# A mixer's triangular solve with its projections, loads and banks ordered anew, ahead of a mixture of experts

## Time and profile before

| | us |
|---|---|
| median of 3 runs | 1212.01 |
| the profiled execution's own time | 1214.35 |
| its span, first to last instruction | 1212.4 |
| TensorE busy in the span | 1187.4 (98%) |
| VectorE, ScalarE, GpSimd busy | 440.9, 259.5, 44.7 |
| DMA, mean over the span | 360 GB/s |
| TensorE clock granted | 0.998 |

### The profile page before, as it was taken

The page is one execution under the profiler, slowest core; times in us unless marked ns, Lnnn a source line. Parts: engine busy times, 40 slices in busy tenths (PEclk is TensorE's granted clock), DMA queues, the critical chain, the costliest instruction groups (busy, mean ns, idle before and its releaser), DMA issues.

```text
span 1212.4 us, 18239 instructions
## 1 busy us (share of the span) xinstructions
PE 1187.4 (98%) x7814; PEld 572.9 (47%) x7814; DVE 440.9 (36%) x962; ACT 259.5 (21%) x630; POOL 44.7 (4%) x101
## 2 busy tenths in 40 slices
PE   8999999999999999999999999999999999999996
PEld 6777677745344344444443444344444444343332
DVE  3357954753413332332233132313322323232324
ACT  3114435422221111111121212021111111111213
POOL 8000110100000000000000000000000000000000
PEclk9999999999999999999999999999999999999999
DMA  9732302498999999999999999999999999999996
GB/s 285 183 105 71 122 31 72 125 414 334 409 426 429 426 414 428 426 432 431 431 429 431 431 431 432 431 426 431 429 432 432 430 430 431 432 432 428 422 424 231
DMA packets 49387, 436.09 MB, mean 360 GB/s; under 512 B 11525, under 2 KB 26952, under 8 KB 31770
## 3 DMA queue, kind: packets, MB, share of 16 engines
q1 hardware_dynamic: 48180, 431.74, 86.4%
q0 software_dynamic: 960, 3.02, 0.8%
q10 hardware_dynamic: 166, 0.15, 0.0%
HBM read 430.01 MB, written 4.89 MB: 359 GB/s over the span
## 4 chain that ended last, share of the span: by engine, by line
PE 86%; DMA 10%; DVE 2%; issue 1%; SPq 0%; ACT 0%; DVEq 0%
PE bank L1634 33%; PE bank L1670 16%; PE bank L914 9%; PE bank L1600 7%; DMA ring<-in_w_gate_up 5%; PE bank L1704 4%; PE bank L1395 3%; DMA ring<-in_w_down 3%; PE bank L1661 3%; DMA mix<-in_w_gate_up 2%; PE bank L1695 1%; PE bank L1152 1%; PE bank L901 1%; PE bank L947 1%; DMA hx<-in_state_shift 0%
## 5 line engine op out<-in xcount | busy, mean ns | idle before, releaser
L1634 PE MATMUL bank<-ring,mix 128*64 128x512 f32 x1504 | 344.8, 598 | 3.3 <-DMA ring<-in_w_gate_up 3.1
L1634 PEld LDWEIGHTS bank<-ring,mix 128*64 128x64 f32 x1504 | 101.3, 136 | 201.0 <-issue 197.7
L1670 PE MATMUL bank<-ring,mix 128*64 128x512 f32 x736 | 168.2, 598 | 0.8 <-DMA ring<-in_w_down 0.8
L2986 DVE TENSOR_TENSOR hTb<-bank,w2a 128x512 f32<-128x512 f32 x32 | 22.1, 692 | 361.3 <-PE bank L1661 361.3
L914 PE MATMUL bank<-hTb,ring 128*128 128x328 f32 (+1 forms) x416 | 120.6, 444 | 0.0
L2218 ACT ACTIVATE mix<-bank,nf 128x256 f32<-128x256 f32 x64 | 26.8, 470 | 431.3 <-PE bank L1600 431.2
L1634 PE MATMUL bank<-mix 128*64 128x512 f32 x500 | 112.7, 595 | 1.8 <-DMA mix<-in_w_gate_up 1.8
L3046 DVE TENSOR_TENSOR mix<-mix,bank 128x512 f32<-128x512 f32 x70 | 48.2, 688 | 159.5 <-PE bank L1704 143.5
L914 PEld LDWEIGHTS bank<-hTb,ring 128*128 128x128 f32 x416 | 77.8, 192 | 33.8 <-issue 2.0
L1670 PEld LDWEIGHTS bank<-ring,mix 128*64 128x64 f32 x736 | 49.3, 136 | 89.9 <-issue 84.0
L1634 PEld LDWEIGHTS bank<-mix 128*64 128x64 f32 x500 | 35.1, 137 | 71.7 <-issue 70.0
(11 more groups left out here) (448 smaller groups left out, 1086.7 us busy)
## 6 DMA issues: line engine op xcount, KB each, us to landing
ring<-in_w_gate_up SPq DMA_DIRECT2D x30, 4096.0 KB, 22.9
ring<-in_w_gate_up SPq DMA_DIRECT2D x33, 2048.0 KB, 14.4
ring<-in_w_down SPq DMA_DIRECT2D x15, 4096.0 KB, 23.7
mix<-in_w_gate_up SPq DMA_DIRECT2D x10, 4096.0 KB, 23.7
ring<-in_w_down SPq DMA_DIRECT2D x14, 2048.0 KB, 13.8
mix<-in_w_gate_up SPq DMA_DIRECT2D x11, 2048.0 KB, 13.2
mix<-in_w_down SPq DMA_DIRECT2D x5, 4096.0 KB, 25.0
ring<-in_w_in SPq DMA_DIRECT2D x14, 1024.0 KB, 5.5
```

What stands on the lines that cost most here:

```text
L1634: last_ = mm(b_[64 * half:64 * half + 64, :].rearrange("s (p q) -> s p q", q=4), toks, cols[:, half], start=(c == 0), stop=(c == KT - 1))
L1670: last_ = mm(b_[r:r + 64, :], lhs, w[:, o:o + NCOL], start=(j == 0 and q == 0), stop=(j == 1 and q == 3))
```

## The change

- `w_out`'s second half is loaded ahead of ring piece 6 instead of after piece 14.
- The unit matrices are copied by ScalarE, behind the raw copy of projection 22, and no longer by GpSimd.
- Gram M's samples go to bank 0 (last used by a stage long read), gT's second part, the fourth unit of the turned states and gT's samples change banks with them.
- Projection 25 is cut 4, 2 and 2 steps, with W(1) ahead of the last two. Projection 28 is cut 5 and 3, with W(3) between. Projection 29 is cut 4 and 4, with Z(4), Us and gram Rk between.
- R0 comes ahead of the a-tokens, on TensorE and on ScalarE. ScalarE copies `us` before projection 29; VectorE gates projection 29 after bk_scaled and gram Rk.

```diff
@@ psum_units
-    add("gM", 3, (2, 3, 1))
+    add("gM", 3, (2, 3, 0))
     add("gN", 3, (4, 5, 6))
-    add("gT", 2, (7, 0))
-    add("s0t", 4, (5, 6, 7, 0))
-    add("gT", 1, (1,))
+    add("gT", 2, (7, 1))
+    add("s0t", 4, (5, 6, 7, 1))
+    add("gT", 1, (0,))
...
     add("Z", 3, (5, 6, 7))
+    add("W", 3, (0, 1, 2))
     end("proj", 25)
-    add("W", 3, (0, 1, 2))
...
-    add("proj", 1, (3,))
+    add("proj", 1, (3,), ended=False)
     add("W", 2, (4, 5))
+    end("proj", 28)
     add("T", 2, (6, 7))
...
-    add("proj", 1, (6,))
+    add("proj", 1, (6,), ended=False)
     add("Z", 2, (4, 5))
     add("Us", 1, (1,))
     add("gRk", 3, (2, 3, 4))
+    end("proj", 29)
+    add("R0", 2, (7, 0))
     add("atok", 2, (5, 6))
-    add("R0", 2, (7, 0))
@@ sync
+                if n == 6:
+                    load(wo[1], w_out[:, 4:8, :], "x1_wo1_in")
                 if n:
                     load(slot(n), w_in[:, :, 512 * g + 256 * u:512 * g + 256 * u + 256], f"ring{n % NSLOT}")
...
-            load(wo[1], w_out[:, 4:8, :], "x1_wo1_in")
@@ gpsimd
-            pool.wait_ge(S("rw_ready"), 1)
-            g.tensor_copy(hx[:, 0:2 * W5].rearrange("p (x t) -> p x t", t=64), mC[:, 6:7, :].broadcast_to([P, 2 * W5 // 64, 64]))\
-                .then_inc(S("eye_ready"), 1)
@@ tensor
-            proj_part(25, 4, KT)
+            proj_part(25, 4, 6)
             make_w(1)
+            proj_part(25, 6, KT)
             make_t(1)
...
-            proj_part(28, 0, KT)
+            proj_part(28, 0, 5)
             make_w(3)
+            proj_part(28, 5, KT)
             make_t(3)
...
-            proj_part(29, 0, KT)
+            proj_part(29, 0, 4)
             make_z(4)
...
             gram("gRk", rk, rr)
-            tokens("atok", rkk, 2)
+            proj_part(29, 4, KT)
             b = [free("R0", 0), free("R0", 1)]
...
+            tokens("atok", rkk, 2)
             pe.wait_ge(S("bk_scaled"), 2)
@@ scalar
+                if n == 22:
+                    act.wait_ge(S("rw_ready"), 1)
+                    a(hx[:, 0:2 * W5].rearrange("p (x t) -> p x t", t=64), mC[:, 6:7, :].broadcast_to([P, 2 * W5 // 64, 64]), ACT.Copy)\
+                        .then_inc(S("eye_ready"), 1)
...
-                if n == 29:
                     ready(cp(us[:, :, :], wait_filled("Us", 0)[:, 0:256].rearrange("p (j v) -> p j v", v=RN)), "Us")
             masked(1)
-            for tile in range(2):
-                b = wait_filled("atok", tile)[:, :].rearrange("p (j g x) -> p g j x", j=4, g=2)
...
             for p in range(2):
                 b, o = wait_filled("R0", p)[:, :].rearrange("p (x v) -> p x v", v=RN), RA[:, p, :, :, 0:64].rearrange("p a j x -> p (a j) x")
...
+            for tile in range(2):
+                b = wait_filled("atok", tile)[:, :].rearrange("p (j g x) -> p g j x", j=4, g=2)
@@ vector
             take_z(4)
-            gate_tile(29)
             dve.wait_ge(S("unit_filled"), U("gRk", 3))
...
             set_masked("gRk", Rk_, 9, 11)
+            gate_tile(29)
```

More of the change, by code:

```diff
@@ L604, in _ @@
                 params(nm, A[src].rearrange("a (h p) -> (a h) p", p=P))
+            w_out = A["w_out"][0].rearrange("(c p) n -> p c n", p=P)
             for n, (g, u) in enumerate(WORDER):
@@ L632, in _ @@
                              A["norm_ffn"][0].rearrange("(j p r) -> p j r", p=P, r=r), "router_in")
-            w_out = A["w_out"][0].rearrange("(c p) n -> p c n", p=P)
-            load(wo[1], w_out[:, 4:8, :], "x1_wo1_in")
             sync.wait_ge(S("unit_filled"), U("proj", 28))
@@ L2134, in _ @@
                         ready(own_rows(e, rRs, 0), "Rs")
-                if n == 29:
                     ready(cp(us[:, :, :], wait_filled("Us", 0)[:, 0:256].rearrange("p (j v) -> p j v", v=RN)), "Us")
             masked(1)
-            for tile in range(2):
-                b = wait_filled("atok", tile)[:, :].rearrange("p (j g x) -> p g j x", j=4, g=2)
-                for g_ in range(2):
-                    ins = cp(RA[:, g_, tile, :, 64:128], b[:, g_])
-                ready(ins, "atok")
             for p in range(2):
@@ L2149, in _ @@
                     ready(cp(o, b), "R0")
+            for tile in range(2):
+                b = wait_filled("atok", tile)[:, :].rearrange("p (j g x) -> p g j x", j=4, g=2)
+                for g_ in range(2):
+                    ins = cp(RA[:, g_, tile, :, 64:128], b[:, g_])
+                ready(ins, "atok")
             ready(cp(bks[:, :, :, :].rearrange("p s j v -> p (s j v)"), wait_filled("bks", 0)[:, :]), "bks")
```

## The result

The changed kernel takes 1216.02 us (median of 15 executions, 1214.35 to 1220.72), the kernel before, beside it on the same chip, 1212.41 us (15 executions, 1210.91 to 1215.73). The ratio is 1.0033, with a 95% interval of 1.0024 to 1.0041: slower by 3.6 us, and inside the 0.5% that the prediction called "within". The forecast was 1212.3, from 1208.3 to 1215.6, so the median lies 0.4 us beyond the range. The kernel before came out 0.4 us above the median that the forecast was built on, so the forecast change, +0.25 us, is missed by 3.4 and its upper end, +3.6, is where the change came out. The profiled execution took 1217.76 us with a span of 1216.1, 1.7 above the median.

A forecast was written before the change was run, and what follows sets the result against it. TensorE's path to Y0, which starts the DMA-bound weight stream, was taken as the bound; −2.9 (front), −0.4 (projection 25), +0.9 (28) and +2.65 (29) gave +0.25 us on 1212.01: 1212.3 us, range 1208.3 to 1215.6.

The forecast's parts named there:

- Z(0)'s page: TensorE's 1.40 us stop in Z(0), taken as a late instruction fetch: 0 to 1.7 us stay, 0.4 taken.
- gram K's page against T(1): Splitting projection 25 removes gram K's 0.85 us stop but T(1) newly waits 0.4 to 0.6: 0.4 us won.
- W(3)'s page against Rs's: Splitting projection 28 puts a 1.3 us instruction-fetch wait at W(3) in place of the 1.12 in Rs.
- second update waits for the a-tokens: Second state update waits for ScalarE's a-tokens: could start at 214.6 us, starts at 217.0 where it was 213.13.
- the one for projection 29: Cutting projection 29 and putting R0 ahead of the a-tokens delays the second state update: 2.65 us lost (1 to 3.5).
- The term for the splits of 25 and 28: Projection 25 cut around W(1), 0.4 us won; projection 28 cut around W(3), 0.9 us lost.
- the front: Gram M through Z(0), with w_out's load, unit matrices and banks changed: 2.9 us won (1.6 to 3.3).
- (1): Rival: faster, 1206.4 to 1210 us, as the tail's new waits don't come; chance 0.27.
- (2): Rival: 1214.9 us; Z(0)'s fetch 3.6 us late, front gives 1.6, split of 25 gives 0, tail takes 4.5; chance 0.15.
- (3): Rival: mid-run stops belong to the work, not instruction pages, so 1.40, 0.85 and 1.12 stay: 1213.7 us; chance 0.10.
- (4): Rival: SyncE's start hangs on state outputs, not Y0: 1212 to 1215 us; chance 0.08 including anything overlooked.
- The reason given for late fetches, thick transfers: Instruction fetches beside heavy DMA traffic start 3.6 us after block entry, against 0.5 otherwise, as at Z(0).

The follow-up runs named there:

- undo29: The changed kernel with projection 29 in one piece and the a-tokens before R0 again: ratio 0.9984 to the kernel before, gram M to stream start 90.73 us.
- filled_short: The changed kernel with six thrown-away products of 216 columns filling TensorE's wait at the second state update: 1216.74 us, ratio 1.0030 to the kernel before.
- pages_shifted: The kernel before with 32 small thrown-away products ahead of projection 23, putting later TensorE instructions 128 further on: 1226.45 us.
- wo1_only: The kernel before with only w_out's second half loaded ahead of ring load 6: one execution, 93.21 us from gram M to stream start (93.66 before).
- front_only: The kernel before with only w_out's earlier load, the unit matrices on ScalarE and the grams' bank changes: 1209.61 us, ratio 0.9973.
- after_again: The changed kernel run once more, unaltered: 1217.52 us, ratio 1.0031 to the kernel before.
- mask_early: The changed kernel with ScalarE's eight masked rows put ahead of the us copy: 1212.80 us, ratio 0.9996 to the kernel before.
- filled_wait: The changed kernel with three thrown-away products of 448 columns filling TensorE's wait at the second state update: 1215.78 us, ratio 1.0026 to the kernel before.
- eye_only: The kernel before with only the unit matrices copied by ScalarE: one execution, 92.35 us from gram M to stream start (93.66 before).
- only29: The kernel before with only projection 29's cut and its new tail order: one execution, 1222.69 us, 103.79 us from gram M to stream start.

## Why the prediction was wrong

Its frame held: the stream's start moves the end one for one, SyncE waits for Y0, all that counts is TensorE's way to it, and ring load 6 was never waited for. Its own sign of being wrong, a start of the stream above 240 us, came (240.32). Point by point:

| term | forecast | measured in the stops of the traced execution |
|---|---|---|
| gram M, turned states | 1.68 and 0.22 gone | 1.68 gone, 0.21 stays |
| Z(0)'s page | 0.4 left of 1.40 | 0.55 |
| gram K's page against T(1) | 0.85 gone, 0.4 to 0.6 new | 0.85 gone, 0.61 |
| W(3)'s page against Rs's | 1.3 for 1.12 | 0.68 for 1.12 |
| first state update waits | some 0.95 new | 0.73 |
| fourth state sum, Z(4) | some 0.5 new | 0.33 |
| second update waits for the a-tokens | 2.4 new | 2.41, and 13.7 us of half clock |
| W(4)'s 0.37 | swallowed | swallowed |
| clock | not in the sum | about 5.7 |

The waits were right to 0.6 us each. The step that failed is the one for projection 29, "**2.65 lost** (1 to 3.5)". It priced the wait of 2.4 us as its own length only. `undo29` against the changed kernel puts the part at 5.3 us of the median (1.7 below before against 3.6 above) and 8.2 of the stretch. The term for the splits of 25 and 28 was short as well: +0.5 forecast (−0.4 and +0.9), +1.4 in the medians and 1.8 in the stretch. The new order by itself was right in the traces: `filled_short`, which has neither the half clock nor a late block in gram Rk, has a stretch 2.65 longer than `undo29` (93.38 to 90.73). Two things were missing. First the clock: 5.7 us in the traced execution (98.95 − 93.66 is 5.3 for 0.4 less of stops), shown by `filled_short` to be the clock's and not the wait's. In the median it is worth about 0.8 us. Second, a late block in gram Rk that 29's cut brings in four traces of seven; the prediction counted the blocks that the change moves at the front and at W(3), and did not go on counting behind the cut.

The clue to the first lay in the trace of before only in part: stops of 1.68 and 1.40 us there left the clock at 1.00, and nothing showed what one of 2.4 does. It was an unknown cost and had to be bounded; instead it was left out of the sum and of the range. That the median missed the range by only 0.4 us is luck in part: seven of the 15 executions lost hardly any clock, and the front won a little more than forecast.

Of the **rivals**, (1) stopped at the tail: its new waits came. (2) had the right sign and came nearest for the tail (4.5 us for the 5.3 of the median) and for the split of 25 (0), but its cause was not there: Z(0)'s fetch started at 146.2 us, 2.7 after its block was entered, and the front gave all it promised. (3), that the stops belong to the work, fell: in the changed kernel gram K's and Rs's stops are gone, and `pages_shifted` moved them all. The rule that spoke for it, the Trainium skill's (Runtime: NRT & Kernel Launch, Instruction fetch mechanics) that a block's crossing is "mostly hidden", holds for 14 of the 20 crossings of this stretch in the trace of before; at the others 0.1 to 1.4 us are seen, and up to 3.5 in `pages_shifted`. (4) fell because SyncE's wait in the changed kernel ends with Y0's fill (L1543), as before.

The reason given for late fetches, thick transfers, is only half of it. At Z(0) the fetch starts 3.6 to 4.3 us after its block is entered in the seven traces with w_out's load beside it, and 2.5 to 3.1 in eleven where the load is moved; in `wo1_only`, where TensorE enters the block later, it is 0.7, and in `pages_shifted`, with other work in the block, 2.9 beside the load. At W(3) no run moved the transfers. And in gram Rk a fetch came 5.9 us late beside idle DMA engines.

The front was sized about right for the median, 2.9 us for 3.1, and too low for the stretch, 4.7. Of the 4.7, the stops explain 3.9 (6.2 us of them in before, 2.35 in `front_only`): 1.68 and 1.18 of Z(0)'s went as named, and the later ones shrank too, which the sum did not count. The other 0.8 us were not traced to a place.

**What stays open.** That the cut of 29 costs these 5.3 us of the median is shown; how they divide is not. They are matched in size, up to a rest, by three parts: the order of the tail, 2.65; gram Rk's block, 1.0 on the mean (some 1.7 us in four of seven traces); the clock, 0.8 in the median (`after_again` against `filled_short`, a difference within their intervals). That leaves 0.9, and `mask_early` points the same way: 3.0 us under `filled_wait` for 1.9 us less of the wait, which leaves 1.1. It is a sum over single traces and no proof. Against before the traces are kinder than the medians: the stretch has `front_only` 4.4 below the mean of before's three (93.42) and `undo29` 2.7, for 3.1 and 1.7 in the medians, and the two filled kernels 1.2 above on the mean, for 3.1 and 3.4. Where these 1 to 2 us lie was not found. Why a block is fetched late beside idle DMA engines is open as well.

Of the versions with more than one execution the best is `front_only`, 1209.61 us, better than both kernels: the load of w_out among the first weights, the unit matrices on ScalarE, the banks, and all projections as before.

## What to carry to other kernels

Price a new stall of TensorE of over 2 us in a dense stretch with what the clock may do behind it, and give the range that end; better, look for work to put into it or for the order that avoids it. Where TensorE executes many small products, number its instructions, and see what stands at the crossings of 256 before and after an edit: taking a wait away brings the next crossing nearer to its fetch. A split of a large step that fills one gap moves every engine that reads its end, so follow that read through each of their queues before it is cut.

## What the runs showed of the hardware

**The clock around a stop.** In the stretch studied all six stops of 2.0 us or more (2.01, 2.41, 2.41, 2.42, 2.83, 3.51) came with a fall from 2.4 to 1.2 GHz, for 3.4 us at 2.01 (`eye_only`), 6.9 at each of the two of `pages_shifted`, and 13.7 at the three of 2.4 us. In four of the six the clock fell 0.3 to 1.0 us before TensorE went on, in `eye_only` and the changed kernel's first trace 1.2 us after. Of the sixteen stops of 1.39 to 1.85 us three were followed by one (1.68 in `only29` and 1.69 in `wo1_only`, 6.9 us; 1.85 in `after_again`, 3.4 us), and thirteen were not (1.85 in `filled_wait`, 1.68 and 1.40 in before). The same stop of 1.85 us in the same gram left the clock alone once and halved it once. What the half clock costs is shown once by a pair of traces whose other stops differ by 0.3 us at most: 5.6 us for 13.7 us of it.

**Fetches of instructions.** At the stops of 0.2 us or more that stand at a block's crossing, the lone fetch had started 0.4 to 5.9 us after TensorE entered the block before, and TensorE went on 2.2 to 2.7 us after its start in the stretch studied.

**GpSimd beside VectorE.** A copy of 2560 columns on GpSimd stretched an operation of VectorE on 8 columns from 0.17 to 2.11 us. It ended with the copy (143.66 and 143.64 us).
